# Reciprocal roots of the normalisations in a two-block transformer kernel: a power on GpSimd in the place of a logarithm and an exponential on ScalarE

## The reference

```python
def rms_norm(x, g, eps=NORM_EPS):
    y = xf * lax.rsqrt(jnp.mean(xf * xf, axis=-1, keepdims=True) + eps)
    return (y * g.astype(jnp.float32)).astype(x.dtype)

def head_rms_norm(x, g, n_heads):          # the same for each head
def layer_norm(x, g, b, eps=1e-5):         # the same after the mean is taken off

def first_block(x, ...):
    for l in range(DEPTH):
        h = rms_norm(x, norm_mix_g[l])
        p = h @ w_in[l]
        y_a = conformer_conv(...)           # ends in layer_norm
        y_b = head_rms_norm(moba_attention(...), moba_out_g[l], MOBA_HEADS)
        y_c = head_rms_norm(gla_chunked(...), gla_out_g[l], GLA_HEADS) * jax.nn.silu(p[..., o6:])
        x = x + jnp.concatenate([y_a, y_b, y_c], axis=-1) @ w_out[l]
        h = rms_norm(x, norm_ffn_g[l])
        ...                                 # convolved, gated feed-forward part
    return rms_norm(x, final_g)

def second_block(x, c, ctx, ...):
    for l in range(DEPTH):
        mod_x = ada_params(c, w_ada[l], b_ada[l])
        x = swiglu_half_step(x, norm_g[l, 0], mod_x, 0, ...)
        hx = modulate(rms_norm_2(x, norm_g[l, 1]), ...)
        ...                                 # q and k of every head go through rms_norm_2 too
        x = swiglu_half_step(x, norm_g[l, 2], mod_x, 6, ...)
```

## Time and profile before

| | before |
|---|---|
| time, median of 3 runs | 3069.34 us (3065.69 to 3071.61) |
| profiled execution, its own time | 3061.71 us |
| its span, first to last instruction | 3059.9 us |
| mean granted TensorE clock | 0.889 |
| TensorE matmul busy | 2657.5 us (87%) |
| VectorE busy | 1617.6 us (53%) |
| ScalarE busy | 1050.3 us (34%) |
| GpSimd busy | 77.2 us (3%) |
| ACT_TABLE_LOAD at L872 and at L874 | 19 and 19, 1.283 us each |

### The profile page before, as it was taken

One profiled execution on the slowest core, in us unless ns is written; L12 is line 12 of the kernel. 1 busy time (PEld: TensorE's weight loads), 2 busy tenths in 40 slices (PEclk: granted clock), 3 DMA queues, 4 the chain that ended last, 5 costly groups with the idle time before them and its releaser, 6 DMA issues.

```text
span 3059.9 us, 39437 instructions
## 1 busy us (share of the span) xinstructions
PE 2657.5 (87%) x15612; PEld 2312.5 (76%) x15612; DVE 1617.6 (53%) x2580; ACT 1050.3 (34%) x1422; POOL 77.2 (3%) x149
## 2 busy tenths in 40 slices
PE   6678889579889999999656899999999998865999
PEld 5578889479787888879533678887788888844999
DVE  4757888558865565742443345744333334333554
ACT  3335634246534222231233233122331223123553
POOL 0000000000000000000000000000000000000000
PEclk9769999579989999998786789999899998768999
DMA  5324574135552453521000124532222222100454
GB/s 211 109 96 159 193 260 152 69 111 192 191 195 103 146 191 137 179 83 42 1 1 1 56 90 144 200 131 90 76 89 98 98 94 90 35 1 1 145 183 147
DMA packets 98005, 350.80 MB, mean 115 GB/s; under 512 B 10577, under 2 KB 13777, under 8 KB 97617
## 3 DMA queue, kind: packets, MB, share of 16 engines
q1 hardware_dynamic: 77136, 273.43, 25.4%
q0 software_dynamic: 20736, 75.51, 7.2%
HBM read 347.85 MB, written 1.05 MB: 114 GB/s over the span
## 4 chain that ended last, share of the span: by engine, by line
PE 73%; DVE 16%; ACT 7%; issue 3%; DMA 0%; SPq 0%; ACTq 0%; DVEq 0%
PE half L508 19%; PE half L510 19%; PE half L509 19%; PE half L619 3%; DVE PROD L1068 2%; PE half L627 2%; DVE U L1403 2%; ACT PR L904 2%; PE half L589 2%; DVE W_lo L1079 2%; PE half L564 2%; ACT W_hi L865 2%; DVE PR L1171 1%; PE half L842 1%; PE half L554 1%
## 5 line engine op out<-in xcount | busy, mean ns | idle before, releaser
L1079 DVE TENSOR_TENSOR W_lo<-W_raw,W_hi 128x1024 fp32r<-128x1024 f32 x510 | 622.5, 1224 | 868.2 <-ACT W_hi L865 866.6
L508 PE MATMUL half<-H_hi,W_lo 128*128 128x256 f32 (+1 forms) x2848 | 961.4, 338 | 57.6 <-DVE H_lo L1131 19.0
L509 PE MATMUL half<-H_lo,W_hi 128*128 128x256 f32 (+1 forms) x2848 | 951.8, 334 | 0.0
L510 PE MATMUL half<-H_hi,W_hi 128*128 128x256 f32 (+1 forms) x2848 | 951.0, 334 | 0.0
L865 ACT ACTIVATE W_hi<-W_raw 128x1024 fp32r<-128x1024 f32 x510 | 536.8, 1058 | 1162.2 <-PE half L510 1092.2
L508 PEld LDWEIGHTS half<-H_hi,W_lo 128*128 128x128 f32 x2848 | 550.9, 193 | 126.8 <-issue 28.9
L510 PEld LDWEIGHTS half<-H_hi,W_hi 128*128 128x128 f32 x2848 | 551.8, 194 | 50.5
L509 PEld LDWEIGHTS half<-H_lo,W_hi 128*128 128x128 f32 x2848 | 552.7, 194 | 48.6
L508 PE MATMUL half<-HID_hi,W_lo 128*128 128x256 f32 (+1 forms) x1056 | 356.6, 338 | 19.9 <-DVE W_lo L1079 17.5
L509 PE MATMUL half<-HID_lo,W_hi 128*128 128x256 f32 (+1 forms) x1056 | 356.0, 337 | 0.0
L510 PE MATMUL half<-HID_hi,W_hi 128*128 128x256 f32 (+1 forms) x1056 | 356.0, 337 | 0.0
(11 more groups left out here) (166 smaller groups left out, 2215.8 us busy)
## 6 DMA issues: line engine op xcount, KB each, us to landing
W_raw<-wstream SPq DMA_DIRECT2D x510, 512.0 KB, 3.2
A_raw<-adastream POOLq DMA_DIRECT2D x144, 512.0 KB, 3.6
CON<-const SPq DMA_DIRECT2D x1, 1025.5 KB, 8.7
X<-xT SPq DMA_DIRECT2D x1, 1024.0 KB, 5.7
X<-ctxT SPq DMA_DIRECT2D x1, 1024.0 KB, 14.8
SC<-cond SPq DMA_DIRECT2D x1, 1024.0 KB, 11.1
outT<-X SPq DMA_DIRECT2D x1, 1024.0 KB, 4.8
PAR<-par SPq DMA_DIRECT2D x1, 684.0 KB, 11.0
```

Source lines behind the costliest of these rows:

```text
L508: pe.matmul(out, wl, xh, start=start, stop=False, skip_group_check=True)
L509: pe.matmul(out, wh, xl, start=False, stop=False, skip_group_check=True)
L510: return pe.matmul(out, wh, xh, start=False, stop=stop, skip_group_check=True)
L1079: dve.tensor_tensor(W_lo[:, v % RING, :], W_raw[:, v % RING, :], W_hi[:, v % RING, :].bitcast(F32), ALU.subtract).then_inc(S.w_lo, 1)
```

## The change

`rstd0` goes from ScalarE to GpSimd. There it is one instruction, a tensor_tensor with the operation pow, of V_ and a tensor EXPO that holds -0.5 everywhere. L_ and its semaphore go away; R0, the Newton step and all else on VectorE and TensorE stay. GpSimd's program, up to now the clearing of AT and the 144 transfers, becomes a walk through the plan: at each stage it issues the transfers whose slots come free by the end of that stage (`ada_after` counts how many reductions VectorE has then made), and then makes the powers of that stage, each behind a wait for its V_.

```diff
+def ada_after(st, n):
+    if st.kind == "mods":
+        return max(n, MODS * st.l + 3 * KT * (st.which + 1))
+    if st.blk == 2:
+        if st.l:
+            return n
+        return max(n, min(n + {"up": 2 * st.pairs, "down": 2 * st.pairs}.get(st.kind, 0), ADA_UNITS))
+    return max(n, min(n + {"up": st.pairs, "down": st.pairs, "out": 4, "att1": 8}.get(st.kind, 0), MODS))
...
-        L_ = sb("L_", [P, 112])
+        EXPO = sb("EXPO", [P, 112])
...
         @block.gpsimd
         def _(pool):
             pool.memset(AT[:, :, :], 0.0).then_inc(S.at_zero, 1)
-            for t in range(ADA_UNITS):
-                wait(pool, S.mod_sums, t - ADA_RING + 1)
-                pool.dma_start(A_raw[:, t % ADA_RING, :], adastream[P * t:P * t + P, :])\
-                    .then_inc(ada_in[t % ADA_RING], 16)
+            pool.memset(EXPO[:, :], -0.5).then_inc(S.at_zero, 1)
+            pool.wait_ge(S.at_zero, 2)
+            loaded = 0
+
+            def ada_loads(upto):
+                nonlocal loaded
+                for t in range(loaded, min(upto, ADA_UNITS)):
+                    wait(pool, S.mod_sums, t - ADA_RING + 1)
+                    pool.dma_start(A_raw[:, t % ADA_RING, :], adastream[P * t:P * t + P, :])\
+                        .then_inc(ada_in[t % ADA_RING], 16)
+                    loaded = t + 1
+
+            def rstd0(rs, n):
+                pool.wait_ge(S.var, rs + 1)
+                pool.tensor_tensor(R0[:, 0:n], V_[:, 0:n], EXPO[:, 0:n], ALU.pow).then_inc(S.rstd0, 1)
+
+            summed = 0
+            for st in PLAN:
+                summed = ada_after(st, summed)
+                ada_loads(summed + ADA_RING)
+                if st.kind in ("norm", "final"):
+                    rstd0(st.rs, st.N // P)
+                if st.kind == "att1":
+                    rstd0(st.rs, 2)
+                    rstd0(st.rs + 1, 8)
+                    rstd0(st.rs + 2, 8)
+                if st.kind == "att2":
+                    rstd0(st.rs, 2 * len(qk_cols(st)))
...
         def _(act):
-            def rstd0(rs, n):
-                act.wait_ge(S.var, rs + 1)
-                act.activation(L_[:, 0:n], V_[:, 0:n], ACT.Ln).then_inc(S.log_var, 1)
-                act.wait_ge(S.log_var, rs + 1)
-                act.activation(R0[:, 0:n], L_[:, 0:n], ACT.Exp, scale=-0.5).then_inc(S.rstd0, 1)
```

More of the change, by code:

```diff
@@ L247, in __init__ @@
         self.stats = new("stats")
+        self.rstd = new("rstd")
         self.var = new("var")
-        self.log_var = new("log_var")
         self.rstd0 = new("rstd0")
-        self.rstd = new("rstd")
         self.rstd_b = new("rstd_b")
@@ L883, in norm @@
                 act.activation(SQ[:, h:KT, 0:N], X[:, h:KT, 0:N], ACT.Square).then_inc(S.squared, 1)
-                rstd0(st.rs, N // P)
                 if st.kind == "final":
@@ L965, in att1 @@
                 act.activation(SQA[:, 0:2, :], AC[:, :, :], ACT.Square).then_inc(S.squared, 1)
-                rstd0(st.rs, 2)
                 act.wait_ge(S.evac, st.tok + 5)
                 act.activation(SQA[:, 2:4, :], OM[:, :, :], ACT.Square).then_inc(S.squared, 1)
-                rstd0(st.rs + 1, 8)
                 act.wait_ge(S.evac, st.tok + 8)
                 act.activation(SQA[:, 4:8, :], OG[:, :, :], ACT.Square).then_inc(S.squared, 1)
-                rstd0(st.rs + 2, 8)
                 act.wait_ge(S.ln_out, l + 1)
@@ L1039, in att2 @@
             def att2(st):
-                rstd0(st.rs, 2 * len(qk_cols(st)))
                 groups(groups2(st))
```

## The result

The changed kernel took 3073.09 us, the kernel before 3065.19 us, medians of 20 runs each. The ratio is 1.0033, with a 95% interval of 1.0025 to 1.0041: the change costs 10 us (8 to 13). The forecast was 8 us less; the rival in which the wide powers eat the gain is the one that came.

A forecast was written before the change was run, and what follows sets the result against it. VectorE's 19 waits between V_ and T_, 34.3 us, were taken as on the chain. GpSimd's 16.2 fixed plus 9.8 for columns, 26.0 us, replace them: 8.3 less, 3069.3 to 3061.0 us; 8-in-10 range 3049 to 3105.

The forecast's parts named there:

- the rival in which the wide powers eat the gain: Two att2 powers, 176 of 244 columns, make the kernel slower; deciding at 0.074 us a column; chance 0.33.
- the part of the power that grows with the columns: GpSimd's 19 powers: about 0.04 us a column, 9.8 us for 244 columns.
- The fixed parts: Each V_ to T_ gap: 0.85 us for the ways there and back and the instruction, 16.2 us for 19.
- The way from VectorE to GpSimd: Before each power: 0.30 us, taken from a transfer that waits for VectorE's last accumulator read.
- The instruction's own part: Fixed part of a GpSimd power: 0.50 us, between a memset's 0.10 and a transfer's 0.53.
- the 17 narrow ones: Normalisations of 2, 4 and 8 columns, 68 columns in all: 17.2 us against 30.4, a gain of 13.2.
- The wide two: att2 normalisations of 104 and 72 columns: 5.0 against 1.96 us and 3.7 against 1.90, a loss of 4.9.
- What was costed at nothing: Effects off the V_ to T_ chain, such as hidden table loads, earlier att1 squares and queued modulation loads: 0 us.
- ScalarE's loads: All 38 table loads of logarithm and exponential go, and most of 21 at the rounding; those off the chain 0 us.
- that buys nothing: In att1 the squares of the next normalisation come sooner, but TensorE takes up their sums right behind its spread: 0 us.
- The modulation loads behind the new waits: GpSimd's next loads queue behind its wait for V_, yet nothing comes late: 0 us.
- No cost is paid once: Rival: code fetched at the first power, in the first norm; at 5.3 us the sum would be -3.0; chance 0.05.

The follow-up runs named there:

- the shift: Changed kernel plus one unused tensor behind EXPO, moving everything allocated after it 448 bytes a partition further on; ratio 1.0077 to the kernel before.
- act_arsqrt: Kernel before with the single ScalarE function Abs_reciprocal_sqrt in place of logarithm and exponential, Newton step kept; ratio 0.9908, 3035.70 us.
- act_sqrt: Kernel before with a square root on ScalarE and a reciprocal on VectorE in place of logarithm and exponential; ratio 0.9929.
- narrow_pool_2: Changed kernel with the two wide roots back on ScalarE, 17 narrow powers on GpSimd, L_ behind the arena; ratio 0.9954 to the kernel before.
- pieces: Changed kernel with each wide att2 normalisation in four pieces, powers begun while TensorE sums later columns; ratio 0.9973 to the kernel before, 3055.92 us.
- loads_back_2: Changed kernel with logarithm and exponential also made on ScalarE into an unread tensor, L_ behind the arena; ratio 1.0047 to the kernel before.
- wide_pool_2: Changed kernel with the 17 narrow roots back on ScalarE, two wide powers on GpSimd, L_ behind the arena; ratio 1.0105 to the kernel before.

## Why the prediction was wrong

The mechanism was the right one. The gaps between V_ and T_ decide, and a microsecond in them is about one of the time: from 5.3 to 59.5 us of gaps the times of the kernels without the shift run from 28 us below to 32 us above the kernel before. Each time in the table has an interval of some 2 to 6 us to either side.

| kernel | gaps, us | less or more than 34.3 | time by its ratio, us |
|---|---|---|---|
| act_arsqrt | 5.3 | -29.0 | -28 |
| act_sqrt | 10.4 | -23.9 | -22 |
| narrow_pool_2 | 23.2 | -11.1 | -14 |
| pieces | 25.9 | -8.4 | -8 |
| changed kernel, two measurements | 48.4 | +14.1 | +10, +13 |
| loads_back_2 | 48.4 | +14.1 | +14 |
| wide_pool_2 | 59.5 | +25.2 | +32 |

The step that failed is the part of the power that grows with the columns. The prediction took 0.04 us a column, by a count of steps at the speed of a memset, and called it a choice and its weak place; it is 0.16. Its 9.8 us for 244 columns are 39. That alone turns -8.3 into +21. The product with the same operands, at 0.002 us a column, shows that even a neighbour with two inputs on this engine would not have given the figure. The stated range, 3049 to 3105 us, holds the 3073, because it reached up to a column at 0.22; the forecast itself has the wrong sign.

The fixed parts were overrated. The way from VectorE to GpSimd was taken as 0.30 us, from a transfer that waits; for the power it is 0.09 (V_ ends at 33.21, the power starts at 33.30), and 0.08 to 0.09 for all 19. The instruction's own part was 0.50 and is 0.40. A gap without its columns is thus 0.52 us, not 0.85, 9.9 us for 19 instead of 16.2, which gives back 6. So 9.9 + 39 = 48.9 by terms, 48.4 by the trace, where 26.0 was forecast.

By width the forecast for the 17 narrow ones was 17.2 us, and they take 19.3 (48.4 less the wide ones' 29.1); their gain was to be 13.2 and is 11.1. The wide two were to cost 8.7 and cost 29.1, so a loss of 4.9 became one of 25.2. Both signs were right, and only the second size was far off. The rival of the wide powers had put its point of decision at 0.074 us a column, and at the fixed parts measured it lies at (34.3 - 9.9) / 244 = 0.10; 0.16 is beyond either.

What was costed at nothing held, nearly. ScalarE's loads went away as forecast (38, and 14 of the 21), and putting them back changed the time by no more than its noise. But "that buys nothing", of the squares that come sooner in `att1`, was right only at the old pace: with the faster power the squares would otherwise be 0.28 us late, twice, as loads_back_2 shows. The modulation loads behind the new waits came in time: GpSimd issues the last one ahead of the first `att1` normalisation at 175.57 and starts the power at 178.74, 3.2 us later. No cost is paid once: the first power takes 0.72 us, as the other seven of its width (0.70 to 0.72).

Between the gaps and the time stay a few microseconds either way. By the gaps the changed kernel should be 14 us slower, and it is 10 (8 to 13); wide_pool_2 is 7 above its gaps. The profiles of single executions differ by up to 4.5 and 6.6 us in the two `att2` stretches, with no order that follows the gaps, and what does it was not tried; nor what makes a `down` stage without the shift run at 117.7 ns now and then.

## What to carry to other kernels

Before work is moved to an engine whose price for it is unknown, measure it at its widest use, not at its commonest: here 17 uses gained 0.05 to 0.98 us each and two lost 25 together. Look first at which of the costs stands on the chain: of the 1.79 us here 1.28 were a table load that one function in the place of two takes off the chain without any other engine. And hold the layout still in an experiment: a tensor more in SBUF moved the changed kernel by as much as the change did, two others by 7 and 9 us and a fourth not at all, and it made a hidden cost look like a real one until the control with nothing but the shift was run.

## What the runs showed of the hardware

- A power in GpSimd's tensor_tensor takes about 0.40 us and 0.16 a column of 128 partitions; a product of the same operands 0.19 us at 2 columns and 0.40 at 104.
- VectorE's signal reaches a waiting tensor_tensor on GpSimd in 0.08 to 0.09 us (19 powers); a waiting transfer started 0.30 us after it in the row read.
- TensorE's products of 128x128 by 128x256 on HID come every 113.4 ns in most stages (23 of 27) with the tensor in one place, and every 118.7 to 120.0 ns in all 15 with it 448 bytes a partition further on, at a granted clock of 1.00 (2.4 GHz) in both. Products of 512 columns on it (232.8 to 232.9 ns) and those of 256 columns on H (119.6 to 119.7) do not change. What in the place does it is open.
- ScalarE's load for Abs_reciprocal_sqrt or Sqrt is issued ahead of the wait of its instruction, like the logarithm's (at 26.92 and 26.89 us, where V_ is over at 33.25 and 33.23): with either function the gap from V_ to the instruction behind it is 0.27 us.
